# Three-branch products of an attention head signalled one by one, and the mixing-output projection started with two tiles side by side

## The reference

```python
y_a = mla_branch(...) @ w_br_a[l]
y_b = pool_branch(...) @ w_br_b[l]
y_c = sgu_branch(...) @ w_br_c[l]
y_d = conv_branch(...) @ w_br_d[l]
gates = jax.nn.sigmoid(gate_logits)
merged = (gates[:, :, 0] * y_a + gates[:, :, 1] * y_b
          + gates[:, :, 2] * y_c + gates[:, :, 3] * y_d)
x = x + rmsnorm(merged @ w_out[l], g_post_mix[l])
```

## Time and profile before

| | |
|---|---|
| time, median of 3 runs | 2702.69 us (2697.7 to 2702.8) |
| time of the profiled execution | 2700.08 us |
| its span, first to last instruction | 2698.3 us |
| PE busy | 2577.9 us, 96% |
| POOL busy | 1799.4 us, 67% |
| DVE busy | 1152.7 us, 43% |
| ACT busy | 581.7 us, 22% |
| DMA, mean | 93 GB/s |
| mean granted TensorE clock | 0.963 of full |

### The profile page before, as it was taken

How to read it: one execution, slowest core, us unless ns; L and a number is a source line. 1 busy time by engine, 2 the same in 40 slices (tenths; PEclk the granted TensorE clock), 3 DMA queues, 4 the chain that set the end, 5 groups by cost and what they waited for, 6 DMA issues and landing times.

```text
span 2698.3 us, 34529 instructions
## 1 busy us (share of the span) xinstructions
PE 2577.9 (96%) x11928; PEld 2076.2 (77%) x11928; DVE 1152.7 (43%) x1582; ACT 581.7 (22%) x996; POOL 1799.4 (67%) x816
## 2 busy tenths in 40 slices
PE   7989999999999899999999999989999999899999
PEld 5867777688887676777768888768887777688887
DVE  3654444544464464443354455554314753311100
ACT  2132311211101113322121110141313431211100
POOL 5756678588887475667758888624431347588887
PEclk9999999999999899999999999889987999999999
DMA  3222222223354222222222335401111212223233
GB/s 119 92 64 86 78 86 94 70 93 97 120 203 156 64 86 65 84 79 91 87 70 93 101 125 204 170 28 58 56 47 55 79 55 86 71 95 100 93 114 104
DMA packets 70211, 250.83 MB, mean 93 GB/s; under 512 B 8304, under 2 KB 8432, under 8 KB 70000
## 3 DMA queue, kind: packets, MB, share of 16 engines
q1 hardware_dynamic: 66816, 241.74, 26.9%
q10 hardware_dynamic: 3312, 7.95, 0.9%
HBM read 247.56 MB, written 2.10 MB: 93 GB/s over the span
## 4 chain that ended last, share of the span: by engine, by line
PE 66%; issue 12%; POOL 10%; DMA 7%; DVE 3%; ACT 1%; SPq 0%; POOLq 0%; DVEq 0%; ACTq 0%
PE bank L461 15%; PE bank L457 15%; PE bank L458 15%; DMA w_raw<-weights 7%; POOL w_lo L383 5%; POOL w_hi L380 5%; PE bank L411 3%; PE bank L413 3%; PE bank L412 3%; PE bank L684 1%; PE bank L928 1%; PE bank L483 1%; PE bank L417 1%; PE bank L418 1%; PE bank L419 1%
## 5 line engine op out<-in xcount | busy, mean ns | idle before, releaser
L380 POOL TENSOR_TENSOR w_hi<-w_raw,one 128x1024 fp32r<-128x1024 f32 x405 | 779.2, 1924 | 858.3 <-PE bank L461 516.6
L383 POOL TENSOR_TENSOR w_lo<-w_raw,w_hi 128x1024 fp32r<-128x1024 f32 x405 | 1022.0, 2523 | 31.7
L457 PE MATMUL bank<-act_hi,w_hi 128*128 128x512 f32 x1840 | 732.5, 398 | 21.2 <-DVE acc L1771 9.5
L458 PE MATMUL bank<-act_lo,w_hi 128*128 128x512 f32 x1840 | 721.5, 392 | 0.0
L461 PE MATMUL bank<-act_hi,w_lo 128*128 128x512 f32 x1904 | 470.4, 389 | 0.0
L457 PEld LDWEIGHTS bank<-act_hi,w_hi 128*128 128x128 f32 x1840 | 349.1, 190 | 107.0 <-issue 18.2
L461 PEld LDWEIGHTS bank<-act_hi,w_lo 128*128 128x128 f32 x1904 | 357.4, 188 | 74.4
L458 PEld LDWEIGHTS bank<-act_lo,w_hi 128*128 128x128 f32 x1840 | 348.8, 190 | 75.4 <-issue 3.8
L457 PE MATMUL bank<-f_hi,w_hi 128*128 128x512 f32 x528 | 206.8, 392 | 0.0
L458 PE MATMUL bank<-f_lo,w_hi 128*128 128x512 f32 x528 | 206.6, 391 | 0.0
L461 PE MATMUL bank<-f_hi,w_lo 128*128 128x512 f32 x528 | 132.4, 391 | 0.0
(11 more groups left out here) (388 smaller groups left out, 3537.0 us busy)
## 6 DMA issues: line engine op xcount, KB each, us to landing
w_raw<-weights SPq DMA_DIRECT2D x405, 512.0 KB, 3.4
mod_raw<-mods SPq DMA_DIRECT2D x48, 512.0 KB, 4.2
bias<-bias ACTq DMA_DIRECT2D x8, 512.0 KB, 4.1
resid<-x SPq DMA_DIRECT2D x8, 256.0 KB, 5.3
out<-resid ACTq DMA_DIRECT2D x8, 256.0 KB, 4.3
params<-params ACTq DMA_DIRECT2D x2, 534.5 KB, 3.9
ctx_raw<-ctx SPq DMA_DIRECT2D x1, 1024.0 KB, 4.8
second<-second SPq DMA_DIRECT2D x1, 972.5 KB, 6.8
```

Of the source, the lines that this page charges most:

```text
L380: nc.gpsimd.tensor_tensor(w_hi[:, j, :], w_raw[:, j, :], one[:, 0:1].to_broadcast([P, 1024]), ALU.mult)\
L383: nc.gpsimd.tensor_tensor(w_lo[:, j, :], w_raw[:, j, :], w_hi[:, j, :].bitcast(F32), ALU.subtract).then_inc(blocks_split, 1)
L457: mm(out, w_hi[:, slot, tile * P:tile * P + P], rows_hi, start=start, stop=False)
L458: mm(out, w_hi[:, slot, tile * P:tile * P + P], rows_lo, start=False, stop=False)
```

## The change

In the head loop the three small products signal each for itself: the first two count up a new semaphore `branch_done`, the third `blocks_done` as before, and DVE waits for each product where it reads it. In `w_out` the first two output tiles are made together: for each k one product into bank 0 and one into bank 1, after both weight blocks have been split entirely. From the third tile on nothing is changed.

```diff
             def w_out(l, b_out, which, at, odd=0):
                 _, _, _, _, m_hi, m_lo, _ = at
 
-                for m in range(KT):
+                for m in range(2):
+                    free(m, which("out", m, 0, l))
+                take(b_out)
+                take(b_out + 1)
+                for k in range(KT):
+                    pe.wait_ge(mrg_lo_ready, 8 * l + k + 1 + 2)
+                    for m in range(2):
+                        last = product(bank[m][:, :], (m + odd) % 2, k, m_hi[:, k, :], m_lo[:, k, :],
+                                       k == 0, k == KT - 1)
+                        if k == KT - 1:
+                            last.then_inc(blocks_done, 1)
+                for m in range(2, KT):
                     free(m % 4, which("out", m % 4, m // 4, l))
-                    if m == 0:
-                        take(b_out)
-                        for k in range(KT):
-                            pe.wait_ge(mrg_lo_ready, 8 * l + k + 1 + 2)
-                            last = product(bank[0][:, :], odd, k, m_hi[:, k, :], m_lo[:, k, :], k == 0, k == KT - 1)
-                        last.then_inc(blocks_done, 1)
-                    else:
-                        block_product(b_out + m, bank[m % 4][:, :], (m + odd) % 2, m_hi, m_lo, range(KT))
+                    block_product(b_out + m, bank[m % 4][:, :], (m + odd) % 2, m_hi, m_lo, range(KT))
@@ head loop, PE
                             for k in range(2):
                                 last = product(bank[j][:, :], 1, 2 * j + k, br_hi[:, 2 * j + k, :],
                                                br_lo[:, 2 * j + k, :], k == 0, k == 1)
-                        last.then_inc(blocks_done, 1)
+                            last.then_inc(branch_done if j < 2 else blocks_done, 1)
@@ head loop, DVE
-                        dve.wait_ge(blocks_done, b0 + 4)
                         for j in range(3):
+                            if j < 2:
+                                dve.wait_ge(branch_done, 2 * h + j + 1)
+                            else:
+                                dve.wait_ge(blocks_done, b0 + 4)
```

More of the change, by code:

```diff
@@ L294, in build @@
             "staged", "scored", "negmax_ready", "prob_ready", "prob_turned", "prob_t_ready", "pv_done", "acc_ready"))
+        branch_done = sem("branch_done")
         prob_normed, oa_hi_ready, masks_ready = sem("prob_normed"), sem("oa_hi_ready"), sem("masks_ready")
```

## The result

| | before | after |
|---|---|---|
| median | 2698.94 us (7 runs, 2694.93 to 2702.8) | 2708.09 us (7 runs, 2704.68 to 2710.09) |
| profiled execution | 2700.08 us | 2707.47 us |
| its span | 2698.3 us | 2705.7 us |

The changed kernel is slower: the ratio is 1.0034, with an interval of [1.0023, 1.0045], or +9.2 us (+6.2 to +12.1) on 2698.94 us. It lies inside the range of 2704 to 2719 us, 4.9 us under the forecast of 2713.

A forecast was written before the change was run, and what follows sets the result against it. PE, busy 96% of the span, was taken as the bound. Heads -4.2 us and `w_out` +16.2 us gave +12.0 us on 2700.1 us, 2712.1 us; with the runs' median 2.6 us higher, 2713 us was taken, range 2704 to 2719.

The forecast's parts named there:

- The stall ahead of `w_out`: Beginning of `w_out`: PE waits for block `b_out + 1` to be split, standing 5.14 us where 2 us were.
- The stall ahead of the third tile: Third `w_out` tile: block `b_out + 2` needs the slot of `b_out`, released late, so PE stands 1.66 us.
- The clock: Behind each of three stalls at `w_out`'s beginning, PE's clock falls to the lower level, costing 2.1 us each.
- The `w_out` term: Two tiles together at `w_out`'s beginning, three places: +9.9 us at full clock plus 6.3 for lower clock, +16.2 us.
- The heads' term: Earlier branch signals, eight pairs of heads: 0.52 us won each, the staging copy being held behind POOL's split; -4.2 us.
- The sum: Whole kernel: -4.2 us in the heads and +16.2 us in `w_out` make +12.0 us.
- No gain in the heads: Rival, heads: L1774 falls behind POOL's `w_hi`, PE's bank 0 wait moves before the scores; +16.2 us, 2718 us; chance 0.15.
- Full gain in the heads: Rival, heads: DVE keeps its copies ahead of POOL's waiting `w_lo`; -11.5 + 16.2 = +4.7 us, 2706 us; chance 0.14.
- Worse: Rival, heads: POOL comes in between the copies, scores up to 2 us later per pair; +26 us, 2728 us; chance 0.05.
- Faster: Rival, `w_out`: split of `b_out + 1` is through when `merging` ends; 5.5 us won there, 2686 to 2693 us; chance 0.03.

The follow-up runs named there:

- wait-alone kernel: Kernel before, old tile order, plus one PE wait for the split of block `b_out + 1` ahead of the first `w_out` tile: 2705.86 us, ratio 1.0045.
- the mended one: Kernel before with branch signals, earlier second-head staging, and second-tile `w_hi` matmuls (k = 0 to 5) before the first tile's k = 6, 7: 2669.49 us, ratio 0.9915.
- `w_out` alone: Kernel before with only the first two `w_out` tiles made together, branch signals as before: 2711.78 us, ratio 1.0056.
- heads alone: Kernel before with only the separate branch-product signals and DVE's waits for them, `w_out` as before: 2693.05 us, ratio 0.998.
- the two with earlier copies: Kernel before with second-head staging ahead of the turned probabilities: with the branch signals 2684.49 us, ratio 0.9957; without them 2697.38 us, ratio 1.0004.

## Why the prediction was right, and where it was off

*The stall ahead of `w_out`* (5.14 us foretold): right. In the rows of the second layer PE starts 1304.48 - 1299.15 = 5.33 us after `merging`'s last matmul, foretold 5.37, and the idle time there is 4.93. The wait-alone kernel shows that it is this wait, and the mended one that the order of the tiles isn't to blame.

*The stall ahead of the third tile* (1.66 us): right, 1.43 to 1.50 us of idle time, and none where the tiles are made one by one.

*The clock* (2.1 us for each): right on average. Filling the stall took away 6.4 us for three. In the changed kernel the stretches lie 1.3, 1.8 and 2.6 us above the 18.01 us at full clock, 5.7 in all where 6.3 was foretold: one value for each place hides that spread. As foretold, the first layer, at full clock before, fell as well.

*The `w_out` term* (+16.2): measured +15.5 in the stretches of the changed kernel, +16.3 with `w_out` alone, and +15.1 by that kernel's ratio.

*The heads' term* (-4.2): the mechanism was right and the size off. It measured -5.7 in the profile, and -5.4 by the ratio of heads alone. I had put the second and third of DVE's five operations too late: the rows have the second gated product 0.43 us behind the start of its matmul (182.61 to 183.04), not 0.84, and so in all 16 heads. The likely reason is that its wait is carried by the instruction itself (DVE's order shows it: `[waits bank_free1,branch_done]`), while the first stands behind separate waits; no run moves a wait to test it. So L1782 was through at 184.45, 0.07 us before POOL began `w_hi`, and did not hold it. POOL's two splits, and with them the copy and the scores, come 0.2 us sooner than I had them. The rest holds: `w_lo` in between, the copy released 0.28 us after its end (186.50 + 2.73 = 189.23, copy until 189.51), the scores 0.90 us after that. PE stands for 0.7 us ahead of them (its block's 24 matmuls from 184.21 end at 189.71, the scores start at 190.41), foretold 0.9. Between pairs the edit was put at nothing, and from a pair's second scores to the next pair's first it is 26.37 to 26.40 us, as before.

The Trainium skill's rule that I weighed in the prediction (SBUF — State Buffer, Who interferes with whom: VectorE's copies in a two-port mode and GpSimd lock each other out for a whole instruction) agrees with the 2.51 us copy, though no view tells in which mode it ran; the 16 short copies of the earlier trace rows, by which the heads would have given 11.5 us, showed only that no POOL split had stood in their way.

*The sum* (+12.0): measured +9.2 [+6.2, +12.1]. Of the difference of 2.8 us, 1.5 us are the heads and 0.7 the stretches; the rest lies inside the interval, and phases of lower clock elsewhere may be in it. With one profile for each kernel these aren't settled. Heads alone shows such a phase: its first-layer stretch took 15.00 us with the same `w_out` code that took 13.71 before, since the clock fell behind the 2 us wait there, which it had not done. The forecast of 2713 lies 4.9 us above the median measured; the other 2.1 us are its base, 2713 - 12.0 = 2701 us, where the kernel before then had a median of 2698.94. None of these errors hid another: all of them lie to the same side, and together they stay inside the range.

*The rivals.* No gain in the heads (2718) falls by heads alone, whose interval ends below 1. Full gain in the heads (2706) can't be told from the forecast by the time alone (2708.09 lies between), but the long copies exclude it. *Worse* falls by the same rows: each pair's scores came 0.2 us sooner than foretold, not later (and its price was summed wrongly: 12.0 + 8 x 2 = 28 us, not 26). *Faster* falls by the 4.93 us wait.

## What to carry to other kernels

Before a wait is put ahead of work, ask what releases it: here the second block's slot was that of the last block just used, so the splitting engine could not start before PE ended, and a 2 us wait became 5 us; using two slots in turn then also gives both back late. To fill a stall, take the part of the next work whose operands are there already (here the `w_hi` products of the six ready tiles), and keep releasing one slot as early as before. And when one engine is freed earlier, follow the next thing that it needs: a 0.4 us copy that starts earlier can land behind another engine's lock, and moving it to where its engine is idle doubled the gain.

## What the runs showed of the hardware that was not expected

- 22 matmuls whose result nobody reads, put into a 5 us wait, kept the granted clock at 1.00 and shortened the stretch by 2.1 us on average (18.01 to 18.02 us three times against 19.81, 20.12 and 20.51), though nothing waited for came sooner.
- Behind a wait of 2 us the clock fell in most cases. Four profiled kernels keep the old `w_out` (before, heads alone and the two with earlier copies): in the second layer and the second block it fell all eight times, in the first layer once in four (stretches of 15.00 and 13.71 us with the same `w_out` code). Behind one of 4.9 us it fell all nine times that the profiles of the changed kernel, `w_out` alone and the wait alone show.
- A waiting POOL split gets in between two VectorE instructions that lie a few hundredths of a microsecond apart: L1784 ended at 185.46 + 1.50 = 186.96 and the copy was due at 187.00, but ended 0.28 us after `w_lo`; so in all eight pairs. Where VectorE's instructions follow each other without a gap, the split stays out: in the kernel before, one `w_hi` starts at 1931.98, beside VectorE operations that end at 1933.84, and takes 3.62 us in place of 1.90.
- From the start of the matmul that it waited for, a VectorE instruction that carries its wait itself began after 0.43 us, one behind separate waits after 0.83 to 0.84 us (16 heads of the changed kernel).
